# Splitting products with a 128-column stationary operand and 64 moving columns into two of 64 stationary columns

## The reference

```python
def step(state, inp):
    r_t, w_t, k_t, v_t, kk_t, a_t = inp
    sa = jnp.einsum('bhij,bhj->bhi', state, -kk_t)
    state = (state * w_t[:, :, None, :]
             + sa[..., None] * (kk_t * a_t)[:, :, None, :]
             + v_t[..., None] * k_t[:, :, None, :])
    y_t = jnp.einsum('bhij,bhj->bhi', state, r_t)
    return state, y_t
```

## Time and profile before

| | us |
|---|---|
| median of 3 runs | 859.2 |
| lowest, highest | 858.9, 860.84 |
| the profiled execution's own time | 860.79 |
| its span | 858.6 |
| PE busy in it | 835.2 |

### The profile page before, as it was taken

The page is one execution under the profiler, slowest core; times in us unless marked ns, Lnnn a source line. Parts: engine busy times, 40 slices in busy tenths (PEclk is TensorE's granted clock), DMA queues, the critical chain, the costliest instruction groups (busy, mean ns, idle before and its releaser), DMA issues.

```text
span 858.6 us, 12164 instructions
## 1 busy us (share of the span) xinstructions
PE 835.2 (97%) x4633; PEld 672.2 (78%) x4633; DVE 412.1 (48%) x596; ACT 332.6 (39%) x508; POOL 117.7 (14%) x124
## 2 busy tenths in 40 slices
PE   5999999999999999999999999999999999999996
PEld 4677767788888777777888898888888888888885
DVE  5479769452453544544662654444444444222215
ACT  6568332232323533435432444444444444211122
POOL 3053870221222201100320000000000000000000
PEclk9999999999999999999999999999999999999999
DMA  6421341421125122123344143333333332222222
GB/s 190 138 74 49 76 145 50 111 56 34 38 67 167 50 75 74 50 74 99 98 161 157 31 142 98 98 98 95 95 93 93 92 101 92 99 97 97 98 74 98
DMA packets 122426, 79.97 MB, mean 93 GB/s; under 512 B 15041, under 2 KB 110322, under 8 KB 122386
## 3 DMA queue, kind: packets, MB, share of 16 engines
q1 hardware_dynamic: 122194, 79.39, 31.0%
q0 software_dynamic: 192, 0.02, 0.0%
HBM read 74.15 MB, written 5.24 MB: 92 GB/s over the span
## 4 chain that ended last, share of the span: by engine, by line
PE 90%; DVE 5%; ACT 3%; DMA 1%; issue 1%; POOL 0%; SPq 0%; ACTq 0%; POOLq 0%; DVEq 0%
PE PS L1526 26%; PE PS L1528 25%; PE PS L1527 25%; PE PS L1622 2%; PE PS L1876 1%; PE PS L1887 1%; PE PS L1899 1%; DVE sq L1196 1%; DVE w_lo L1122 1%; PE PS L1729 1%; PE PS L1768 1%; PE PS L1769 1%; PE PS L1747 1%; PE PS L1807 1%; DMA xt<-in_x_dram 1%
## 5 line engine op out<-in xcount | busy, mean ns | idle before, releaser
L1526 PE MATMUL PS<-hT_hi,w_hi 128*128 128x512 f32 (+2 forms) x688 | 270.7, 393 | 3.4 <-DVE hT_lo L1146 1.3
L1528 PE MATMUL PS<-hT_hi,w_lo 128*128 128x512 f32 (+2 forms) x688 | 263.2, 382 | 0.0
L1527 PE MATMUL PS<-hT_lo,w_hi 128*128 128x512 f32 (+2 forms) x688 | 263.1, 382 | 0.0
L1122 DVE TENSOR_TENSOR w_lo<-wraw,w_hi 128x1024 fp32r<-128x1024 f32 (+1 forms) x125 | 163.2, 1307 | 154.0 <-ACT w_hi L767 151.7
L767 ACT ACTIVATE w_hi<-wraw 128x1024 fp32r<-128x1024 f32 (+1 forms) x125 | 131.3, 1050 | 130.0 <-PE PS L1528 106.3
L1526 PEld LDWEIGHTS PS<-hT_hi,w_hi 128*128 128x128 f32 (+1 forms) x688 | 128.6, 187 | 36.7 <-issue 10.2
L1528 PEld LDWEIGHTS PS<-hT_hi,w_lo 128*128 128x128 f32 (+1 forms) x688 | 128.7, 187 | 26.5
L1527 PEld LDWEIGHTS PS<-hT_lo,w_hi 128*128 128x128 f32 (+1 forms) x688 | 128.8, 187 | 24.6 <-issue 1.0
L1526 PE MATMUL PS<-w_hi,act_hi 128*128 128x512 f32 x176 | 68.5, 389 | 0.0
L1528 PE MATMUL PS<-w_hi,act_lo 128*128 128x512 f32 x176 | 68.5, 389 | 0.0
L1527 PE MATMUL PS<-w_lo,act_hi 128*128 128x512 f32 x176 | 68.5, 389 | 0.0
(11 more groups left out here) (241 smaller groups left out, 1040.3 us busy)
## 6 DMA issues: line engine op xcount, KB each, us to landing
wraw<-in_w_ffn_in_dram SPq DMA_DIRECT2D x88, 256.0 KB, 3.0
wraw<-in_w_in_dram SPq DMA_DIRECT2D x82, 256.0 KB, 3.1
wraw<-in_w_ffn_out_dram SPq DMA_DIRECT2D x44, 256.0 KB, 2.8
wraw<-in_w_o_dram SPq DMA_DIRECT2D x16, 256.0 KB, 3.0
xt<-in_x_dram SPq DMA_DIRECT2D x4, 512.0 KB, 5.3
qk_scratch<-stage SPq DMA_DIRECT2D x8, 256.0 KB, 3.0
qkT<-qk_scratch SPq DMA_DIRECT2D x4, 512.0 KB, 4.4
wraw<-in_w_up_a_dram SPq DMA_DIRECT2D x8, 256.0 KB, 2.9
```

The lines of the kernel that those rows point to most:

```text
L1122: dve.tensor_tensor(w_lo[:, q, 0:n], wraw[:, s, 0:n], w_hi[:, q, 0:n].bitcast(F32), ALU.subtract)\
L1526: pe.matmul(out_, a_hi, b_hi, start=start, stop=False)
L1527: pe.matmul(out_, a_hi, b_lo, start=False, stop=False)
L1528: return pe.matmul(out_, a_lo, b_hi, start=False, stop=stop)
```

## The change

Two helpers are added to TensorE's list. Each issues one product as two, of stationary columns 0 to 63 into output partitions 0 to 63, and of stationary columns 64 to 127 into output partitions 64 to 127, with the same moving operand. All products of `solve` and `outputs` go through them; `state` and the rest are as before. The semaphore increments stay on the last instruction of each group.

```diff
+            def halves(out_, lhs, rhs, start, stop):
+
+                pe.matmul(out_[0:HD], lhs[:, 0:HD], rhs, start=start, stop=stop)
+                return pe.matmul(out_[HD:P], lhs[:, HD:P], rhs, start=start, stop=stop)
+
+            def from_state(out_, lhs, rhs, stop):
+
+                pe.matmul(out_[0:HD], lhs[:, 0:HD], rhs, start=False, stop=stop)
+                return pe.matmul(out_[HD:P], lhs[:, HD:P], rhs, start=False, stop=stop)
...
-                        ins = pe.matmul(PS[:, 4 + odd, i * HD:(i + 1) * HD], LK_rk[:, 4 * odd + i, 0, :],
-                                        V_tok[:, h * HD:(h + 1) * HD], start=i == 0 or c == 0, stop=c == 0)
+                        ins = halves(PS[:, 4 + odd, i * HD:(i + 1) * HD], LK_rk[:, 4 * odd + i, 0, :],
+                                    V_tok[:, h * HD:(h + 1) * HD], start=i == 0 or c == 0, stop=c == 0)
...
-                            ins = pe.matmul(PS[:, 4 + odd, i * HD:(i + 1) * HD], kkE_R[r, i, c, 0, :], S_sb[r, i, :],
-                                            start=False, stop=i == 3)
+                            ins = from_state(PS[:, 4 + odd, i * HD:(i + 1) * HD], kkE_R[r, i, c, 0, :], S_sb[r, i, :],
+                                             stop=i == 3)
...
-                        ins = pe.matmul(PS[:, 6 + half, i * HD:(i + 1) * HD], TmT[:, h, :], G_sb[:, h, :],
-                                        start=True, stop=True)
+                        ins = halves(PS[:, 6 + half, i * HD:(i + 1) * HD], TmT[:, h, :], G_sb[:, h, :],
+                                    start=True, stop=True)
...
-                        pe.matmul(o, LK_rk[:, sh, 1, :], V_tok[:, h * HD:(h + 1) * HD], start=i == 0, stop=False)
-                        ins = pe.matmul(o, MT_rb[:, sh, 1, :], U_sb[:, sh, :], start=False, stop=c == 0 and i == 3)
+                        halves(o, LK_rk[:, sh, 1, :], V_tok[:, h * HD:(h + 1) * HD], start=i == 0, stop=False)
+                        ins = halves(o, MT_rb[:, sh, 1, :], U_sb[:, sh, :], start=False, stop=c == 0 and i == 3)
...
-                            ins = pe.matmul(PS[:, bank, i * HD:(i + 1) * HD], kkE_R[r, i, c, 1, :], S_sb[r, i, :],
-                                            start=False, stop=i == 3)
+                            ins = from_state(PS[:, bank, i * HD:(i + 1) * HD], kkE_R[r, i, c, 1, :], S_sb[r, i, :],
+                                             stop=i == 3)
```

## The result

The changed kernel takes 844.83 us, median of 4 runs (844.01 to 847.73); the kernel before, with one run more than ahead of the prediction, takes 859.99 (858.9 to 860.84, 4 runs). The ratio is 0.9824, with a 95% interval of 0.9809 to 0.9839: 1.8% faster. In a second comparison, further down, it is 0.983 (0.9807 to 0.9853). The forecast was 844.8 within 841.8 to 849.6.

A forecast was written before the change was run, and what follows sets the result against it. The prediction took PE's rate of passes to bound the kernel: 13.4 + 2.4 - 1.4 = 14.4 us saved, from a base of 859.2 to 844.8, range 841.8 to 849.6.

The forecast's parts named there:

- The products with 128 rows: G, T G and y with V and U: 256 passes at 0.111 us become 512 at 0.0292, 13.4 us saved.
- The products with the state: Six groups of 64-row products in three chunks: four array quarters run together, 2.4 us saved, ends -0.2 and 3.4.
- The changes of form: Array switching shape between products in the chunk loop: nine more changes at 0.15, 1.4 us lost, bounds 0 and 2.3.
- The cover: Copies of G and U stay hidden under the fill: nothing lost, 0.1 to 0.4 us to spare at T G.
- the 0.2 of the earlier trace: PE's 0.2 us wait for yc between the first two chunks, which the prediction said stays.
- (a): Rival for the split products: the column halves take turns instead of overlapping, 2.7 us slower, 861.9; chance 4%.
- (b): Rival for the products with the state: the quarters give nothing, 11.8 us saved, so 847.4; chance 17%.
- (c): Rival for long runs in `outputs`: PE can't be fed, a pass costs 0.040, 5.6 us lost, 850.4; chance 8%.
- (d): Rival: copies of G and U come out from under the fill, up to 0.8 in three chunks, 846.8; chance 12%.

The follow-up runs named there:

- e2: The changed kernel with the 128-row products put back to one matmul, only the products with the incoming state split: 858.25 us, ratio 0.9974 to the kernel before.
- e4: The changed kernel with T G left whole, one matmul per product: 848.72 us, ratio 0.9862 to the kernel before.
- e10: The changed kernel with the fill's one step between G and T G moved ahead of the second merge: 847.32 us (one run).
- e3: The changed kernel with the 128-row products' low halves issued in long runs, then the high ones (T G 8 and 8): 857.22 us, ratio 0.9969.
- e1: The changed kernel with the products with the incoming state put back to one matmul, the others split: 848.5 us, ratio 0.9865 to the kernel before.
- e5: The changed kernel with the 128-row products cut into four of 32 stationary columns: 848.61 us, ratio 0.9861 to the kernel before.
- e8: The kernel before with T G's moving operand widened from 64 to 128 columns, for timing only: 859.51 us (one run).
- e9: The changed kernel, T G in halves, with its moving operand widened to 128 columns, for timing only: 847.51 us (one run).

## Why the prediction was right

The time (844.8 for 844.83) is closer than its terms deserve, and that much is luck: the runs of this kernel alone spread over 3.7 us. The loop is the fair test, 14.4 forecast for 14.68. From G to G the second chunk takes 222.27 - 194.18 = 28.09 us, for 230.57 - 198.43 = 32.14 before: 4.05 shorter, at the edge of the 3.5 to 4 that was forecast. The span as a whole fell by 15.6, 1.2 of it ahead of the loop, where the change has no part.

- **The products with 128 rows.** Forecast 13.4 less 1.4 for changes of form, 12.0; measured 12.3 (e2 against the changed kernel). The price of 0.0292 taken from `state` held: T G's 32 passes begin over 0.93 of their 1.08, and e4 gives 2.04 for 2.2. The 0.111 that the prediction put on all former passes is a little high for T G, whose rows gave 0.106; the difference, 64 x 0.005 = 0.3 us, is within what the changes of form leave open.
- **The products with the state.** Forecast 2.4 between -0.2 and 3.4, with no row that showed four places; measured 2.34 and 2.37. The reading from the merge of 32-blocks was the right one, and the Trainium skill's floor of about 25 ns from start to start ("TensorE: Matmul & The Clock Gate", Part 1) does not hold between places: a round of four began within 0.02 us.
- **The changes of form.** 0.15 forecast, 0.13 to 0.17 measured, by the price taken for T G's whole passes. One gain showed where it was counted: 0.15 between `state` and `outputs` in each of three chunks.
- **The cover.** Nothing forecast, nothing seen. In the second chunk the copies of G end 0.5 us ahead of T G's second half (196.75, and 196.78 + 0.46), a little more than the 0.4 that I gave; e10 shows the price once the cover goes. A small gain was missed: the 0.2 of the earlier trace rows didn't stay, 0.12 of it went.
- **The rivals.** (a) was refuted for the order of the helper, and e3 showed that another order brings most of it about: y, G and T G in long runs leave 3.5 of 14.7 us, and 2.4 of these are the products with the state. (b) was refuted by e1 and e2, (c) by the stretches of the changed kernel (y's 64 passes in 2.01 us, with no gap behind them), (d) by the waits (its price, 0.8 in three chunks, is 2.4 us and not the 2 that it was given). The Trainium skill's sentence that weight loads overlap only across row groups (the same page, Part 3) fails for column halves here: lines 1721 and 1722 share all 128 rows, and a load of line 1722 begins at 194.24, while the matmul of line 1721 that began at 194.18 and lasts 0.27 is in flight. The weight loads (PEld) of the changed kernel there:

```profile
194.23 0.14 PEld L1721 LDWEIGHTS PS<-V_tok,LK_rk 128*64 128x64 f32 x1
194.24 0.14 PEld L1722 LDWEIGHTS PS<-V_tok,LK_rk 128*64 128x64 f32 x1
```

- **What the argument lacked.** I priced the pass by a neighbour of the same shape without saying why 64 columns are cheaper than 128. The answer, the larger operand, came from e5, e8 and e9. The number didn't need it; a forecast for another shape would have.

## What to carry to other kernels

Where a float32 product has 128 stationary and 64 moving columns, its pass costs as much here as one with 128 moving columns (e8): half of what it pays for is unused. Cut the stationary operand to the moving one's width, place the pieces in different column halves (and row halves), and issue them by turns, within four passes of each other. Cutting further than the moving operand is wide brought 0.05 us in a stretch of 1.08, and nothing in the loop as a whole. Read the price from start to start, never from durations.

## What the runs showed of the hardware

- A float32 pass holds its place in the array for a time set by its larger operand: 0.106 to 0.112 us with 128 columns, 0.056 to 0.058 with 64, so about (0.111 - 0.058) / 64 = 0.83 ns per column between the two. Widening the smaller one up to the larger costs nothing (e8: 1.70 us as before), beyond it all (e9: 1.90 for 1.08).
- Passes in different column halves, over the same rows and into the same bank, run side by side even when each half has four in a row. In longer runs only about four passes on each side of a turn do, which saves 0.16 to 0.19 us a turn (e3: G 1.83, T G 1.47, y 3.64). At a turn the passes of the second half begin before the last ones of the first, against the order of the list.
- Four quarters of 64 by 64, and four column strips of 128 by 32, all run together: 32 passes in 0.62 us with a change of form, and in the strips a new pass each 0.0139 us over 128 passes.
- To change the array's form costs 0.13 to 0.17 us each time.
